# Weight halves, transposes and one weight sum moved at the entry of a feed-forward block, in a hybrid decoder step

## The reference, cut to what matters

```
mix = concatenate([h_m, h_a])
x = layer_norm(ALPHA * x + mix @ w_out, ln1_g, ln1_b)
ff = (silu(x @ w_gate) * (x @ w_up)) @ w_down
y = layer_norm(ALPHA * x + ff, ln2_g, ln2_b)
```

## Time and profile before

| what | us |
|---|---|
| median of three runs (1548.25 to 1549.83) | 1549.42 |
| the profiled execution, its own time | 1547.07 |
| its span, first to last instruction | 1545.1 |
| PE busy in the span | 1499.2 |
| PE idle before the entry's first product | 2.51 |
| PE idle before the entry's fourth product | 2.01 |
| one weight sum with s = 0 in a down stage | 1.16 |
| the other weight sums there | 0.68 |

### The profile page before, as it was taken

How to read it: one execution, slowest core, us unless ns; L and a number is a source line. 1 busy time by engine, 2 the same in 40 slices (tenths; PEclk the granted TensorE clock), 3 DMA queues, 4 the chain that set the end, 5 groups by cost and what they waited for, 6 DMA issues and landing times.

```text
span 1545.1 us, 28871 instructions
## 1 busy us (share of the span) xinstructions
PE 1499.2 (97%) x11167; PEld 1384.8 (90%) x11167; DVE 955.3 (62%) x2021; ACT 500.2 (32%) x1134; POOL 501.1 (32%) x550
## 2 busy tenths in 40 slices
PE   8999999999999999889999999999999999999998
PEld 8996799999997766588779999999999999999986
DVE  3008599999983665474455565656656466565686
ACT  4336533321234566263244212222122221222310
POOL 3630165512210001334246523434234342343430
PEclk9999999999999999999999999999999999999999
DMA  6210231223215301835001101212011120111221
GB/s 192 73 47 16 70 97 43 69 70 103 83 67 187 108 29 43 229 110 175 1 28 56 55 28 56 62 35 69 28 56 61 36 69 28 55 60 38 71 94 72
DMA packets 102070, 110.72 MB, mean 72 GB/s; under 512 B 16650, under 2 KB 89486, under 8 KB 101938
## 3 DMA queue, kind: packets, MB, share of 16 engines
q1 hardware_dynamic: 101298, 106.80, 21.7%
q0 software_dynamic: 640, 2.10, 0.4%
HBM read 88.82 MB, written 19.95 MB: 70 GB/s over the span
## 4 chain that ended last, share of the span: by engine, by line
PE 54%; DVE 2%; POOL 1%; issue 1%; ACT 0%; DVEq 0%
PE bank L2046 26%; PE bank L2096 13%; PE bank L1665 5%; PE bank L2388 3%; PE bank L2069 3%; DVE weight_sum L2186 1%; PE bank L2380 1%; PE bank L1167 0%; PE bank L1854 0%; PE bank L1170 0%; POOL c_and_n_sample L1317 0%; PE bank L1133 0%; PE bank L1153 0%; PE bank L1661 0%; DVE y_acc L2344 0%
## 5 line engine op out<-in xcount | busy, mean ns | idle before, releaser
L1964 POOL TENSOR_TENSOR weight_split<-gate_up,weight_split 128x512 fp32r<-128x512 f32 x128 | 167.6, 1314 | 313.6 <-ACT weight_split L1960 311.8
L2684 PE MATMUL bank<-w_split,xT_split 128*128 128x256 f32 (+1 forms) x1950 | 248.9, 285 | 2.9 <-ACT w_split L2759 1.8
L2684 PEld LDWEIGHTS bank<-w_split,xT_split 128*128 128x128 f32 (+1 forms) x1950 | 235.8, 188 | 7.2 <-issue 3.7
L2046 PE MATMUL bank<-x_split,weight_split 128*128 128x272 f32 (+1 forms) x1920 | 239.9, 284 | 0.0
L2046 PEld LDWEIGHTS bank<-x_split,weight_split 128*128 128x128 f32 x1920 | 236.6, 188 | 0.0
L2096 PE MATMUL bank<-hidden_split,weight_split 128*128 128x352 f32 x1296 | 212.3, 323 | 1.7 <-DVE y_acc L2344 1.5
L2096 PEld LDWEIGHTS bank<-hidden_split,weight_split 128*128 128x128 f32 x1296 | 207.5, 188 | 5.0 <-DVE y_acc L2344 3.8
L2046 PE MATMUL bank<-x_sums,weight_split 128*128 128x256 f32 (+1 forms) x1440 | 181.5, 284 | 0.0
L2046 PEld LDWEIGHTS bank<-x_sums,weight_split 128*128 128x128 f32 x1440 | 177.8, 188 | 0.0
L3022 DVE TENSOR_SCALAR_CACHE_REDUCE chosen<-scores,level 128x384 uint8<-128x384 f32 (+2 forms) x198 | 174.3, 943 | 1.2
L1960 ACT ACTIVATE weight_split<-gate_up 128x512 fp32r<-128x512 f32 x128 | 79.3, 629 | 259.6 <-PE bank L2046 78.6
(11 more groups left out here) (346 smaller groups left out, 2141.5 us busy)
## 6 DMA issues: line engine op xcount, KB each, us to landing
w_unit<-in_w_in_dram SPq DMA_DIRECT2D x15, 1024.0 KB, 5.6
gate_up<-in_w_gate_dram SPq DMA_DIRECT2D x22, 512.0 KB, 3.5
gate_up<-in_w_up_dram SPq DMA_DIRECT2D x22, 512.0 KB, 3.6
down_weight<-in_w_down_dram SPq DMA_DIRECT2D x36, 256.0 KB, 2.7
scratch_dram<-feature_stage SPq DMA_DIRECT2D x36, 176.0 KB, 1.8
scores<-in_x_prompt_dram SPq DMA_DIRECT2D x8, 512.0 KB, 4.2
out_dram<-stage SPq DMA_DIRECT2D x32, 128.0 KB, 1.7
out_weight<-in_w_out_dram SPq DMA_DIRECT2D x16, 256.0 KB, 6.8
```

Of the source, the lines that this page charges most:

```text
L1964: pool.tensor_tensor(slot(e, 1), part_source(e), slot(e, 0).bitcast(F32), ALU.subtract).then_inc(slot_lo, 1)
L2046: mm = pe.matmul(PS[BANK_OF[j] + c][:, 0:CW[c]], slot(e, a)[:, k, :], XPARTS[j][:, b, k, CO[c]:CO[c] + CW[c]], start=(j in BEGINS and k == ...
L2684: mm = pe.matmul(out, tokens, w[:, b, k, :], start=((k, a, b) == terms[0]), stop=((k, a, b) == terms[-1]))
```

## The change

It edits five places. DVE makes the low half of part 1, in the loop over the tiles after the work of t = 7, behind a wait for part 0's low half. POOL makes the low half of part 0 ahead of the low pieces of t = 6 instead of after those of t = 6, and the low half of part 2 ahead of those of t = 7, behind a wait for part 1's. ACT makes the high half of part 0 ahead of the two puts of t = 6, that of part 1 after them. PE transposes t = 8 between the two halves of product 1 instead of after it, 12 matmuls earlier. In the down stages the weight sum with s = 0 stands after m = 11 instead of m = 12. DVE also gets a wait for the low pieces before t = 8, ahead of the last piece which it makes.

```
@@ dve_out
                 if t:
                     highs_of(t - 1)
+                if t == LAST - 1:
+                    dve.wait_ge(slot_lo, 1)
+                    low_part(dve, 1)
             highs_of(LAST)
             dve.wait_ge(x1_hi, lows_before(TILES))
+            dve.wait_ge(x1_lo, lows_before(LAST))
             piece_low(dve, pieces_of(LAST)[1])
@@ pool_x1
-            for t in range(TILES - 2):
+            for t in range(TILES - 3):
                 lows(t)
             low_part(pool, 0)
-            low_part(pool, 1)
+            lows(TILES - 3)
+            pool.wait_ge(slot_lo, 2)
+            low_part(pool, 2)
             lows(TILES - 2)
-            low_part(pool, 2)
             lows(TILES - 1, 1)
@@ act_x1
             for t in range(TILES):
-                if t == LAST:
-                    high_part(act, 1)
+                if t == LAST - 1:
+                    high_part(act, 0)
                 if t:
                     put_turned(2 * t - 2)
...
                 if t == LAST - 1:
-                    high_part(act, 0)
+                    high_part(act, 1)
@@ low_part
-        def low_part(pool, e):
-            pool.wait_ge(slot_hi, e + 1)
-            pool.tensor_tensor(slot(e, 1), part_source(e), slot(e, 0).bitcast(F32), ALU.subtract).then_inc(slot_lo, 1)
+        def low_part(eng, e):
+            eng.wait_ge(slot_hi, e + 1)
+            eng.tensor_tensor(slot(e, 1), part_source(e), slot(e, 0).bitcast(F32), ALU.subtract).then_inc(slot_lo, 1)
@@ first_matrix
                     for f in range(2):
+                        if no == 1 and f:
+                            pe_x1(pe, 2 * LAST)
+                            pe_x1(pe, 2 * LAST + 1)
...
                     mm.then_inc(product, 1)
-                    if no == 1:
-                        pe_x1(pe, 2 * LAST)
-                        pe_x1(pe, 2 * LAST + 1)
@@ down
-                    if m in (12, 15, 18):
-                        weight_sum(dve, 2 * g + 3, (m - 12) // 3)
+                    if m in (11, 15, 18):
+                        weight_sum(dve, 2 * g + 3, (11, 15, 18).index(m))
```

## The result

Six runs of the changed kernel have a median of 1538.77 us (1537.03 to 1542.22), six of the kernel before 1549.62 (1548.25 to 1552.46). The ratio is 0.993 with a 95% interval of 0.9915 to 0.9944: 10.85 us less by the medians, where 10.8 was forecast. The profiled execution took 1538.40, its span is 1536.7.

What follows compares the result with a forecast made beforehand. PE, busy for 97% of the span, was taken to bound the kernel. The entry's 7.1 us (2.51 + 1.6 + 1.45 + 1.5) and the down stages' 3.7 made 10.8: from 1549.42 to 1538.6 us, range 1536.0 to 1543.0.

Steps and rivals of the forecast that it cites:

- First wait, 2.51 + 1.6: Feed-forward entry, ahead of product 0: PE's 2.51 us wait goes, and with it 1.6 us of slow clock.
- 0.8 to spare: Entry: DVE's low half of part 1 ends at 803.1, and up to 803.9 it costs nothing.
- Second wait, 1.45 + 1.5: Entry, ahead of product 3: earlier transposes shrink PE's wait by 1.45, from 2.01 to 0.55; 1.5 us of slow clock goes.
- the one which cost POOL's new order at nothing: Entry: POOL's wait ahead of part 2's low half, holding back t = 7's pieces, is over by 803.1 and costs nothing.
- the margin of 0.9 ahead of the transposes: Entry: t = 8 is centred at 807.41, PE reaches its transposes at 808.3, so 0.9 us is left.
- An idle time of their own: Entry: the prediction is wrong if the transposes have PE idle time of their own ahead of them; no size given.
- The clock's 1.5 behind product 3: Entry, behind product 3: with only 0.55 us of wait left, the clock stays full and 1.5 us is taken back.
- a rival: Entry: the clock falls again at product 3, 1.5 stays lost, 9.3 saved, 1540.1 us; chance 0.12.
- The weight sum, 0.41 a stage: Down stages: after m = 11 the sum takes 0.68 instead of 1.16, saving 0.41 in each of nine, 3.7 us.
- the 0.05 that was left for a late add: Down stages: 0.05 of the 0.46 us stall stays, as the add behind the s = 1 sum is 0.08 late.
- POOL wins the port: Down stages, m = 11: POOL begins before DVE's sum; 8.6 lost, 7.1 gained at the entry, 1550.9 us; chance 0.05.
- the stall only moves: Down stages: the add of m = 12 is late instead of m = 13's; 7.1 remains, 1542.3 us; chance 0.12.

Runs made afterwards that it cites:

- the profile with 52.36: Repeat profile of the changed kernel with t = 8 transposed after product 1 again; entry 52.36 us, execution 1538.91 us; that kernel's median is 1540.28.
- the run with the parts made as before: Changed kernel with the old order of high and low halves for parts 0 to 2 on ACT, POOL and DVE; 1540.80 us, one run.
- the run with part 2 later: Changed kernel with POOL's low half of part 2 after the pieces of t = 7 instead of ahead of them; median 1537.08 us.
- the run with m = 6: Changed kernel with the weight sum s = 0 after m = 6 instead of m = 11; median 1543.87 us.

## Why the prediction was right

**The total.** 10.8 was forecast, 10.57 is what the traces show from the mark on, 10.85 what the medians show. It was made of the terms that were named. That it came so close is luck in part, for two errors cancel: the entry gave 6.49 where 7.1 was forecast, the down stages 4.11 where 3.7 was.

**First wait, 2.51 + 1.6.** The forecast was right. With the transposes at the old place and the fall behind product 3 (the profile with 52.36), 56.68 - 52.36 = 4.32 are saved against 4.1. DVE's low half was held by one POOL piece, as taken: the forecast left 0.8 to spare, 0.54 was left.

**Second wait, 1.45 + 1.5.** The forecast was right by itself (2.96 in the run with the parts made as before), but too large inside the whole change (52.36 - 50.19 = 2.17). The step that failed is the one which cost POOL's new order at nothing: "it is over by 803.1, while POOL still works on t = 6" looked at POOL's wait only, not at whom POOL's low half of part 2 would meet at its new place. It meets the centring at 808.76. This moves the pieces of t = 7 into the first cast of t = 8 (1.05 instead of 0.43 in the run with part 2 later) and POOL's first piece of t = 8 into the second (1.33 instead of 0.46), and leaves 1.23 of the wait instead of 0.55. For the same reason nothing was left of the margin of 0.9 ahead of the transposes. The tile was centred at 810.41, and PE began to transpose it at 810.47, 0.11 later after product 0 than in the run with part 2 later. An idle time of their own there was named as a sign of being wrong. It came, too small for the bracket, and with what followed it cost 5.38 - 5.21 = 0.17; that it was no more was luck.

**The clock's 1.5 behind product 3.** It was gained, but it is no fixed price: behind the wait of 2.01 the clock falls in some executions and not in others. Behind the 1.23 of the changed kernel it stayed at 1.00, and the three other profiles with that wait have the same entry (50.19 to 50.21). Where it doesn't fall behind the 2.01, the moved transposes are worth only 50.83 - 50.19 = 0.64 in this kernel. The prediction's remark that the idle length is no full rule was right; it had put this into a rival instead of into the term.

**The weight sum, 0.41 a stage.** The mechanism was right, the size somewhat low: 0.46 on average, all of the stall; the 0.05 that was left for a late add did not come. The condition, DVE 0.27 ahead of POOL, is what the trace after shows in the same number. The rivals "POOL wins the port" and "the stall only moves" did not come about; the run with m = 6 shows the same loss when DVE meets POOL's running operation elsewhere. A POOL start ahead of DVE at m = 11 was not tried.

## What to carry to other kernels

When an operation is moved to another engine or place, look up what runs beside it there: in these traces of DVE and POOL, who starts first sets the price of both. A wait of the engine that sets the time can cost more than its length through the clock behind it, but whether it does may differ from one execution to the next, so such a term belongs into the range. Where the runs vary more than the effect, count from a mark in the trace just ahead of the change.

## What the runs showed of the hardware

A 128x512 subtraction of float32 on POOL holds up not only DVE operations with two inputs in SBUF (0.68 to 1.16 or 1.53), but also those with one: a cast of 128x512 took 1.33 and a centring of 128x1024 1.65, twice its 0.82. The Trainium skill (SBUF — State Buffer, Who interferes with whom) says that casts and tensor_scalar instructions can run in modes that use both ports, when their operands meet the conditions, and so can contend with GpSimd. These two rows agree with it; the prediction had reckoned only with operations of two inputs. When DVE was first it lost nothing, and POOL's 1.29 became 1.56.

Where DVE started second, the end of its operation can be priced from the end of POOL's: the sums with two inputs, the low half of part 1 and the last piece of t = 8 end 0.55 to 0.56 after it, the centring 0.54, the casts 0.27 and 0.29. Of two POOL pieces in a row, DVE's low half of part 1 waited only for the first, which ended at 804.84: it was done at 805.40, while the second ran from 804.81 and took 1.74.

PE's idle time of 2.0 us was followed by the 1.2 GHz level for a part of the next 3.9 us in one profile (granted clock 0.60) and by the full clock in three others of the same kernel.
